# Norm statistics and rows issued inside neighbouring products, in a two-block transformer kernel on one core

## The reference

```
h = rms_norm(x, norm1_g);  proj = h @ w_in          # first block
q, k = rms_norm(q per head), rms_norm(k per head)   # 8 heads of 64
x = x + mix @ w_out
up = rms_norm(x, norm2_g) @ w_up; conv; silu(gate) * val; x = x + ... @ w_down
h = rmsnorm(x, pre_mix_w);  proj = h @ w_in_2       # second block
merged = g_a * (y_a @ w_branch_a) + g_b * (y_b @ w_branch_b)
x = x + rmsnorm(merged @ w_out_2, post_mix_w)
h = rmsnorm(x, pre_ffn_w)
f = (silu(h @ w_gate) * (h @ w_up)) @ w_down
out = x + rmsnorm(f, post_ffn_w)
```

## Time and profile before

| | |
|---|---|
| Median of 3 runs | 3093.67 us (3091.85 to 3094.84) |
| The profiled execution's own time | 3094.52 us |
| Its span in the trace | 3092.7 us |
| TensorE busy | 2924.6 us, 95% of the span |
| VectorE, ScalarE, GpSimd busy | 46%, 31%, 12% |
| Mean granted TensorE clock | 0.969 |

### The profile page before, as it was taken

How to read it: one execution, slowest core, us unless ns; L and a number is a source line. 1 busy time by engine, 2 the same in 40 slices (tenths; PEclk the granted TensorE clock), 3 DMA queues, 4 the chain that set the end, 5 groups by cost and what they waited for, 6 DMA issues and landing times.

```text
span 3092.7 us, 31280 instructions
## 1 busy us (share of the span) xinstructions
PE 2924.6 (95%) x13012; PEld 2357.9 (76%) x13012; DVE 1434.8 (46%) x1673; ACT 944.8 (31%) x1193; POOL 360.3 (12%) x308
## 2 busy tenths in 40 slices
PE   7988999999999999899999999998978999999995
PEld 5777667788888888688878887666757888888874
DVE  5775554453545454533234444775463213233335
ACT  3212443231312122321246655432332121111123
POOL 2212111000000000200012222113220000000003
PEclk9988999999999999999999999999988999999997
DMA  2123542111111111236423334564421111111113
GB/s 104 62 75 111 135 100 84 59 43 53 46 51 45 52 41 55 85 124 191 157 70 103 97 94 142 152 196 171 160 89 52 40 57 40 56 38 58 50 64 118
DMA packets 88653, 272.09 MB, mean 88 GB/s; under 512 B 12600, under 2 KB 15288, under 8 KB 88512
## 3 DMA queue, kind: packets, MB, share of 16 engines
q1 hardware_dynamic: 74016, 223.71, 22.5%
q0 software_dynamic: 14496, 46.38, 4.3%
HBM read 217.45 MB, written 52.59 MB: 87 GB/s over the span
## 4 chain that ended last, share of the span: by engine, by line
PE 78%; DVE 9%; ACT 4%; issue 3%; DMA 1%; POOL 1%; SPq 0%; DVEq 0%; POOLq 0%; ACTq 0%
PE ps L206 77%; DVE cacc L177 1%; DVE YA L174 1%; ACT PB L171 1%; PE ps L209 1%; ACT AH L171 1%; DVE PB L177 1%; DVE ps L186 1%; DVE stk L174 1%; DVE XT L174 1%; DVE wl L174 0%; ACT wh L171 0%; DVE XR L174 0%; DMA raw<-in_w_w2out 0%; DVE AL L177 0%
## 5 line engine op out<-in xcount | busy, mean ns | idle before, releaser
L206 PE MATMUL ps<-AH,wh 128*128 128x512 f32 (+1 forms) x2240 | 900.6, 402 | 67.3 <-DVE AL L177 25.3
L206 PE MATMUL ps<-AL,wh 128*128 128x512 f32 (+1 forms) x2240 | 882.7, 394 | 0.0
L206 PE MATMUL ps<-AH,wl 128*128 128x512 f32 (+1 forms) x2240 | 881.8, 394 | 0.0
L174 DVE TENSOR_TENSOR wl<-raw,wh 128x1024 fp32r<-128x1024 f32 (+2 forms) x241 | 280.8, 1165 | 834.5 <-ACT wh L171 834.3
L206 PEld LDWEIGHTS ps<-AH,wh 128*128 128x128 f32 (+1 forms) x2240 | 425.1, 190 | 176.7 <-DVE AL L177 36.6
L171 ACT ACTIVATE wh<-raw 128x1024 fp32r<-128x1024 f32 (+2 forms) x289 | 261.8, 906 | 796.0 <-PE ps L206 783.5
L206 PEld LDWEIGHTS ps<-AH,wl 128*128 128x128 f32 (+1 forms) x2240 | 425.6, 190 | 93.0
L206 PEld LDWEIGHTS ps<-AL,wh 128*128 128x128 f32 (+1 forms) x2240 | 426.3, 190 | 90.0 <-issue 3.4
L206 PE MATMUL ps<-UH,wh 128*128 128x512 f32 x880 | 346.6, 394 | 13.6 <-DVE wl L174 8.6
L206 PE MATMUL ps<-UL,wh 128*128 128x512 f32 x880 | 345.1, 392 | 0.0
L206 PE MATMUL ps<-UH,wl 128*128 128x512 f32 x880 | 344.8, 392 | 0.0
(11 more groups left out here) (198 smaller groups left out, 3110.2 us busy)
## 6 DMA issues: line engine op xcount, KB each, us to landing
raw<-in_w_up SPq DMA_DIRECT2D x44, 512.0 KB, 3.2
raw<-in_w_gu SPq DMA_DIRECT2D x44, 512.0 KB, 3.2
raw<-in_w_w2in SPq DMA_DIRECT2D x32, 512.0 KB, 4.2
raw<-in_w_down SPq DMA_DIRECT2D x56, 256.0 KB, 2.6
raw<-in_w_down SPq DMA_DIRECT2D x32, 320.0 KB, 2.8
xin<-in_xT SPq DMA_DIRECT2D x16, 512.0 KB, 4.4
stk<-scr_ka SPq DMA_DIRECT2D x32, 256.0 KB, 8.0
raw<-in_w_w2v SPq DMA_DIRECT2D x16, 512.0 KB, 3.3
```

Of the source, the lines that this page charges most:

```text
L174: return Issued(self, self.e.tensor_tensor(out, a, b, op))
L206: return Issued(self, self.e.matmul(out, l, r, start=start, stop=stop))
```

## The change

- `half_product` and `product` take a function `aside(half, k)`, which is called ahead of each k and may issue other matmuls there.
- First projection: statistics of norm n are issued in half 0 at k = 6 of the next product on the list (k0, q1, cb1, q2, k2, q3, k3 for n = 0 to 6), its rows in half 1 at k = 6. Norm 7 goes behind the first and the second value tile. On VectorE the reciprocal (`inverse`) is taken out of `second`, and the taps are split so that one stands ahead of it. ScalarE squares n+1 ahead of `high(n)`, and `w_high` is moved ahead of `scale_root`. The stores of norms 6 and 7 go one and three tiles later.
- First feed-forward: statistics of norm 2 in the first product, rows in the second.
- Second projection: the first two products are begun with k = 0 to 3 of both, and k = 4 to 7 of both follow. Norm 3 stands inside. The order on ScalarE and VectorE is not changed.
- Last mixture: one piece for each half product, x = 9 to 15, with the last one behind. VectorE's three steps of a piece are taken apart and interleaved with those of its neighbours. Norms 4 and 5 are inside products. The second halves of g0 and u0 take turns, k by k. SyncE's stores and GpSimd's sums follow the new order.
- Second feed-forward: norm 6 goes inside product x = 2, which uses the fourth PSUM pair, and `w_high` and `w_low` of the tile behind it go ahead of its root and reciprocal.

The diff, cut to its core (ScalarE's `w_high(12)` and `scale_root(3)` stand behind `square(3)` in the new code; VectorE's last mixture has `mult`, `add`, `low` and `total` as functions in place of `x3`):

```diff
             if ready:
                 ready(k)
+            if aside:
+                aside(half, k)
             ws = slice(k * m, k * m + m)
             q.mm(out, h[:, ws], hi[k][:, c], first and k == ks[0], False)
...
-        def win(name, m=P):
+        def win(name, m=P, n=None):
+            def scales(half, k):
+                if (half, k) == (0, 6):
+                    qk_stats(n)
+                if (half, k) == (1, 6):
...
-            self.product(q, self.a_tile(name), self.Ah, self.Al, 8, self.a_pair(name), m, lambda k: q.wait_ge(S.xl, k + 1))
...
+                         None, scales if n is not None else None)
+        def qk_stats(n):
             q.wait_ge(S.qsq, n + 1)
             q.wait_ge(S.nsq, 1)
             q.wait_ge(S.qsqrt, n)
             for t in range(NT):
...
                 i = q.mm(self.bank(7)[:, 2 * t:2 * t + 2], self.T1[2][:, t * 128:t * 128 + 128], self.blk, True, True)
             i.then_inc(S.qst)
+        def qk_rows(n):
             q.wait_ge(S.qrc, n + 1)
...
-        win("k0")
-        qk_scales(0)
+        win("k0", P, 0)
         pool_out(1)
-        win("q1")
-        qk_scales(1)
-        win("cb1")
-        qk_scales(2)
+        win("q1", P, 1)
+        win("cb1", P, 2)
         win("ca1")
         win("k1")
         for n, name in ((3, "q2"), (4, "k2"), (5, "q3"), (6, "k3")):
-            win(name)
-            qk_scales(n)
-        qk_scales(7)
+            win(name, P, n)
         def free0(t):
...
             self.value_part(q, 0, kc, (self.Ah, self.Al), 0, free0, TILE["wv", (0, kc)])
+            if kc == 0:
+                qk_stats(7)
+            if kc == 1:
+                qk_rows(7)
...
+        square(1)
         high(0)
-        square(1)
         pool_out(1)
         self.w_high(q, 8)
         scale_root(1)
+        square(2)
         high(1)
-        square(2)
         self.w_high(q, 9)
...
-            scale_root(n - 1)
+            square(n)
             high(n - 1)
-            square(n)
-        scale_root(7)
+            self.w_high(q, n + 9)
+            scale_root(n)
+        wv = TILE["wv", (0, 0)]
+        self.w_high(q, wv + 2)
         high(7)
-        wv = TILE["wv", (0, 0)]
-        for s in range(wv + 1, wv + 5):
+        for s in range(wv + 3, wv + 5):
             self.w_high(q, s)
         for tok in range(4):
...
-        def second(n):
-            b = n % 2
+        def inverse(n):
             q.wait_ge(S.qsqrt, n + 1)
             q.wait_ge(S.qrow, n)
             q.recip(self.rcols[:, 16:32], self.scol[:, 0:16]).then_inc(S.qrc)
+        def second(n):
+            b = n % 2
             q.wait_ge(S.qrow, n + 1)
...
         first(2)
         second(1)
-        taps(self.TAPS["q1"], 31)
+        taps(1, 31)
+        inverse(2)
...
+        taps(self.TAPS["k1"] - 1, 62)
         for n in range(4, 8):
             first(n)
             second(n - 1)
-            taps(5, 62)
+            taps(1, 62)
+            inverse(n)
+            taps(4, 62)
         second(7)
...
-        after = {7: [0], 8: [1], 9: [2], 12: [3], 13: [4], 14: [5], 15: [6, 7]}
+        after = {7: [0], 8: [1], 9: [2], 12: [3], 13: [4], 14: [5], 16: [6], 18: [7]}
         for s in range(1, TILE["wout", 0] + 1):
...
         S = self.S
+        def norm(half, k):
+            if (x, half, k) == (0, 1, 4):
+                q.wait_ge(S.g2a, 7)
+                self.norm_stats(q, 2, self.acc2, 0, NT)
+            if (x, half, k) == (1, 0, 6):
+                self.norm_rows(q, 2, self.rc8, 0, NT)
...
-                q.wait_ge(S.g2a, 7)
-                self.norm_stats(q, 2, self.acc2, 0, NT)
-                self.norm_rows(q, 2, self.rc8, 0, NT)
...
-            q.wait_ge(S.bev, n - 1)
-            self.product(q, TILE["w2in", key], Bh, Bl, 8, n % 2, P, lambda k: q.wait_ge(S.pl, k + 1))
-            if n == 0:
+        def ready(k):
+            q.wait_ge(S.pl, k + 1)
+        def norm(half, k):
+            if (n, half, k) == (0, 1, 4):
                 q.wait_ge(S.pa, 7)
                 self.norm_stats(q, 3, self.acc2, 0, NT)
+            if (n, half, k) == (1, 0, 4):
                 self.norm_rows(q, 3, self.rc8, 0, NT)
+        for part in range(2):
+            for n in range(2):
+                q.wait_ge(S.dev, 39 + n)
+                for half in range(2):
+                    self.half_product(q, TILE["w2in", self.PROJ2[n]], Bh, Bl, 8, half, 2 * n + half, P, ready,
+                                      range(4 * part, 4 * part + 4), part == 0, part == 1, norm)
+        for n in range(2, 16):
+            q.wait_ge(S.bev, n - 1)
+            self.product(q, TILE["w2in", self.PROJ2[n]], Bh, Bl, 8, n % 2)
         for tag, sweep, kc in self.SWEEPS2:
...
+        def norm4(half, k):
+            if (x, k) == (8, 5):
+                q.wait_ge(S.pa, 14)
+                q.wait_ge(S.mx, 192)
+                self.norm_stats(q, 4, self.acc3, 0, 4)
+            if (x, k) == (9, 1):
+                self.norm_rows(q, 4, self.rcols[:, 8:12], 0, 4)
+        def stats5(half, k):
+            if k == 6:
+                q.wait_ge(S.pa, 21)
+                self.norm_stats(q, 5, self.acc3, 4, 8)
+        def rows5(half, k):
+            if k == 2:
+                self.norm_rows(q, 5, self.rcols[:, 12:16], 4, 8)
...
-                    q.wait_ge(S.mx, 192)
-                    self.norm_stats(q, 4, self.acc3, 0, 4)
-                    self.norm_rows(q, 4, self.rcols[:, 8:12], 0, 4)
-        q.wait_ge(S.x3l, 8)
...
-        self.half_product(q, g0, self.Ah, self.Al, 8, 0, 0)
-        q.wait_ge(S.pa, 21)
-        self.norm_stats(q, 5, self.acc3, 4, 8)
-        self.norm_rows(q, 5, self.rcols[:, 12:16], 4, 8)
-        self.half_product(q, u0, self.Ah, self.Al, 8, 0, 2)
...
-        self.half_product(q, u0, self.Ah, self.Al, 8, 1, 3)
+        self.half_product(q, g0, self.Ah, self.Al, 8, 0, 0, P, lambda k: q.wait_ge(S.x3l, k + 1), None, True, True, stats5)
+        self.half_product(q, u0, self.Ah, self.Al, 8, 0, 2, P, None, None, True, True, rows5)
+        for k in range(8):
+            for s, b in ((g0, 1), (u0, 3)):
+                self.half_product(q, s, self.Ah, self.Al, 8, 1, b, P, lambda k: q.wait_ge(S.x3l, 9 + k), [k], k == 0, k == 7)
     def act_out2(self, q):
         S = self.S
-        def scales(half):
-            self.norm_sqrt(q, 4 + half, 4)
+        def rows(half):
             q.wait_ge(S.nrow, 4 + half)
             q.act(self.RB2[:, HALF[half]], self.bank(4 + half), ACT.Copy).then_inc(S.nrb)
...
+                if x == 8:
+                    self.norm_sqrt(q, 4, 4)
+                if x == 9:
+                    rows(0)
...
-                elif half and n <= 4:
-                    x3(2 * n - 2, 0)
-                    x3(2 * n - 1, 0)
+                if half and n:
+                    x3(n - 1, 0)
         self.w_high(q, TILE["gu", ("u", 0)])
-        scales(1)
+        x3(7, 0)
+        self.norm_sqrt(q, 5, 4)
+        rows(1)
         for n in range(NT):
             x3(n, 1)
...
+            c = HALF[half]
+            q.wait_ge(S.xs, 16 + 8 * half)
+            q.wait_ge(S.xacc, 13 + 7 * half)
+            q.tt(self.acc3[:, c], self.acc3[:, c], self.sq3[1][:, c], ALU.add).then_inc(S.xacc)
         for half in range(2):
             c = HALF[half]
             for n in range(NT):
...
                 self.w_low(q, TILE["w2out", (half, n)] + 1)
+                if x == 8:
+                    self.norm_recip(q, 4, self.rcols[:, 8:12], 4)
+                if half and n == 1:
+                    mult(0, 0)
+                if half and n:
+                    mult(n, 0)
+                    add(n - 1, 0)
+                if half and n > 1:
+                    low(n - 2, 0)
                 if n == 7:
                     q.wait_ge(S.ps, 8 + x + 1)
                     q.wait_ge(S.pa, 7 + 7 * half + 6)
                     q.tt(self.acc3[:, c], self.acc3[:, c], self.sq3[1][:, c], ALU.add).then_inc(S.pa)
-                if x == 8:
-                    self.norm_recip(q, 4, self.rcols[:, 8:12], 4)
-                elif half and n <= 4:
-                    x3(2 * n - 2, 0)
-                    x3(2 * n - 1, 0)
+                if x == 15:
+                    add(7, 0)
+                    low(6, 0)
...
+        low(7, 0)
+        total(0)
         self.norm_recip(q, 5, self.rcols[:, 12:16], 4)
+        mult(0, 1)
+        mult(1, 1)
+        add(0, 1)
         for n in range(NT):
-            x3(n, 1)
+            if n < 6:
+                mult(n + 2, 1)
+            if n < 7:
+                add(n + 1, 1)
+            low(n, 1)
+        total(1)
         self.w_low(q, TILE["gu", ("g", 1)])
...
-                if half and 1 <= n <= 4:
-                    for m in (2 * n - 2, 2 * n - 1):
-                        if 1 <= m < 7:
-                            total(m, 0)
+                if half and n > 1:
...
+    def f2_pair(x):
+        return 3 if x == 2 else x % 2
     def u2(self, j0, j1):
...
```

(24 more changed lines are left out.)

68 lines of the change are left out of this document (33 added, 35 removed).

## The result

| | before | after |
|---|---|---|
| Median of 4 runs | 3094.26 us (3091.85 to 3102.24) | 3040.29 us (3039.72 to 3044.77) |
| Ratio, 95% interval | | 0.9824 (0.9804 to 0.9844) |
| The profiled execution's own time, its span | 3094.52, 3092.7 us | 3044.77, 3043.0 us |

The change makes the kernel 54 us faster, 1.8%; 3044 was forecast. Its page, as the earlier trace rows: the busy time of the engines and the chain that ended last.

The account below looks back on a forecast made before the run. TensorE, busy 95% of the span, was taken as the bound, so only its waits and low clock could give time. First projection -13, norm 2 -5, second projection +3, last mixture -35: -50 from 3094.5, 3044 us; range 3032 to 3060.

Parts of the forecast that it names:

- Norm 0 to q2, +3: First projection: TensorE waits 3.5 us for norm 0's square and wakes slow, so q2 begins 3.1 us later; +3 us.
- q2 to the middle, -21: First projection, q2 to the middle of the values: products with norms inside take 14.7 us, not some 17.4; -21 us.
- The clock in it, +5: First projection: statistics' small matmuls lower TensorE's clock, 1 us for each of 5 norms; +5 us, bounds 0 and 9.
- Rival A: Small matmuls cost no clock while no wait is near, so 7 us charged for norms 2 to 7 go: 3037; chance 0.15.
- Norm 2, -5: First feed-forward: waits of 0.60 and 2.44 us, slow rows and 8 slow matmuls go; -5 us, bounds -6.4 and -4.
- the clock's 1.2: Norm 2 in the first feed-forward: 1.2 us charged for a lowered TensorE clock, set against the -6.4 us.
- Second projection, +3: Second projection: a 5.1 us wait for the second product's weights replaces one of 3.06; +3 us, bounds -3 and +5.
- Last mixture, -35: Last mixture to the end of product x = 2: fewer waits, pieces 2.4 us apart; -35 us, bounds -38 and -25.
- some sharing with GpSimd: Last mixture, second-half pieces: VectorE's three instructions of 0.68 us and this sharing make 2.4 us a piece.
- Stages between don't change: Stages between and after the changed ones run dense at clock 1.00 and don't change.
- B: Rival: VectorE becomes the bound of the first projection, its middle comes 10 us later: 3054; chance 0.15.
- C: Rival: the mixture's chain is longer, seven steps lose 9 us and the second half 5 more: 3058; chance 0.08.
- D: Rival: statistics inside products keep the clock low for whole products, 9.6 us for each of 12 norms: 3160; chance 0.02.

Follow-up runs that it names:

- e2: Changed kernel with norm 0's square ahead of the gate's three activations on ScalarE and one VectorE tap moved ahead of its wait for them: 3033.72 us, 0.9802 to before.
- e10: The changed kernel itself, unedited, measured again beside the kernel before: 3037.53 us, 0.9813 to before.
- e4: Changed kernel with the statistics' small matmuls inside q2, k2, q3 and k3 issued 2, 3, 4 and 6 times over: 3076.65 us, one run.
- e5: Kernel before with only the last mixture's part of the change (norms 4, 5 and 6 inside products): 3058.75 us, 0.9880 to before.
- e8: Changed kernel with GpSimd's six additions for the third state's second half done on 8 columns of 512: 3030.81 us, one run.
- e11: Kernel before with only norm 2 inside the first feed-forward products and the second projection's part of the change: 3092.80 us, 0.9990 to before.

## Why the prediction was right or wrong

The total was right within 4 us, the median being below the forecast by 3.7 (by 6.5 in the second measurement). That the profiled execution, at 3044.77, met 3044 so closely is luck: its four stretches gained 56 us where 50 were forecast, and other stretches gave most of the difference back. By its steps:

- **Norm 0 to q2, +3: right.** The wait was 3.27 us (3.5), 12 matmuls behind it were slow (13), and q2 came 3.04 us later (3.1). e2 shows that the square's place is the whole of it. The forecast said that the change leaves the activations ahead of the square, and so priced a defect of the change; it didn't see VectorE's 9.3 us without work.
- **q2 to the middle, -21: right**, -20.7. The taps' end had 11 us of cover and now has 1.2 in this profile, where the forecast said none; in e10 TensorE waits 0.70 us for it. The sum of VectorE's work beside a product was added up wrong, its terms make 13.6 us and not 13.9, which changes nothing here.
- **The clock in it, +5: wrong.** The step that failed is "For 5 norms I charge 1 us each, near half of the 1.75 of rows 7". In the profile of after, no 512-column matmul was slow behind any statistics or rows inside a product but norm 0's, which follow a wait. I had taken the rows for a group of 1.95 us, when 5.47 us of such matmuls stand there in a row, and took one execution's low stretch for a rule. The forecast's words "nothing was idle before it" were right, and e4 shows such a charge, but only from three sets on. Rival A, with 0.15, was the right mechanism for norms 2 to 7 too, though not for groups as long as e4's; its 3037 is nearer to both medians than 3044.
- **Norm 2, -5: the waits right, the clock's 1.2 not needed.** The first profiles say -6.6, where the terms without the clock made -6.4; against e5, where the low clock behind its waits didn't come, it is -3.4.
- **Second projection, +3: right in its mechanism**, 5.18 for 5.1 and the third product late by 0.9 us. Counted from the start of the last down product (1298.16 before, 1274.81 after), the third product starts 1.1 us later, where +2.1 was forecast: seven slow matmuls behind the wait, not 13, and before had 13 behind a shorter one. From the one to the other it is 44.6 to 45.3 us in the seven profiles with half sums and late weights, and 43.5 to 43.9 in the three with the second projection of before.
- **Last mixture, -35: nearly**, -32.9 in the two first profiles and -34.5 in e10's. Two terms were mis-sized and pull against each other. Pieces of the second half took 2.9 us and not 2.4, over seven pieces 3.5 us: "some sharing with GpSimd" was 1.03 us for each piece, in two steps of every second one (e8). Against that, the chain for x = 9 to 15 fits under a half product, so the 1.8 us of waits did not come. The rest is the clock, charged at 1 us for x = 2: the low stretch behind the wait of 1.88 us costs 1.6 in the first profile, and in e10's it didn't come.
- **"Stages between don't change": wrong by a few us either way.** In the profiled execution three stretches gave back 8.8 us (2.8, 3.9 and 2.1, the last by the 5.59 us wait before the gated mixture), and others gained 2, which hid in its span what the clock's 5 had been charged too much. Profiles differ there with the same code: the neighbourhood attention's stretch took 210.6 to 215.6 us over thirteen, and 215.6 was after's. The other three runs of after are 4.4 to 5 us faster.

Little spoke for B, C or D: VectorE kept up in the first projection but for the 0.70 us at the taps' end in some profiles, the mixture's chain was shorter than allowed, and no product ran at the lower clock for its whole length.

## What to carry to other kernels

A wait on the engine that bounds a stretch may have been bought long before: follow the late engine back to its last idle time, and move work from the busy end into it (six taps into 9.3 us of idle time took away a wait of 6.2 us that stood 60 us later). When a product is begun earlier, ask what it needs that stands in a queue behind work for later, and move that first: half sums cost 2 us here with the weights late, and moving the weights gave back 6. A norm's small matmuls inside a product cost their own time and no clock here, so put norms inside products, but don't line up several groups (e4).

## What had not been expected of the hardware

- Small matmuls in a row, without any wait, can lower TensorE's clock. In e4, one execution, it stayed at 1.00 with 32 records (3.63 us), as with 16 (1.84 us), and fell to 0.50 inside the groups of 48, 64 and 96 (5.5 us of work took 8.06), for 8 to 13 large matmuls behind them too.
- Whether the clock falls differs between executions of the same code: behind the same wait of 1.88 us it was 0.50 for 3.4 us in after and 1.00 in e10, and behind the 5.47 us group it fell in before and not in e11 (in five of the thirteen profiles in all).
- GpSimd's addition of two 128x512 operands (1.48 to 1.65 us) holds up a VectorE step beside it by some 1.03 us, more than the step's own 0.74, and the step ends 0.55 us after the addition (six of six). Moving the six additions to VectorE, at 0.6 us each, makes the stretch from g0 to x = 2 4 us shorter.
